# The first weight unit behind each norm of the second block works on inputs without the root

## The reference

```python
def rmsnorm(x, g):
    y = x * lax.rsqrt(jnp.mean(x * x, axis=-1, keepdims=True) + NORM_EPS)
    return y * g
def modulate(x, g, shift, scale):
    return rmsnorm(x, g) * (1 + scale) + shift
# layer 0
x = x + 0.5*gt1 * swiglu(modulate(x, g1, sh1, sc1), ffn1_wi, ffn1_wo)   # and ctx alike
x = x + gt2 * conformer_conv(modulate(x, g2, sh2, sc2), ...)            # 31 taps, LayerNorm, swish
x = x + 0.5*gt3 * swiglu(modulate(x, g3, sh3, sc3), ffn2_wi, ffn2_wo)
# layer 1: the same, with windowed attention in place of the convolution;
# its last two sublayers update x alone
return rmsnorm(x, final_g)
```

## Time and profile before

| | us |
|---|---|
| median of three runs | 3041.43 (3038.14 to 3042.28) |
| the profiled execution | 3040.12 |
| its span | 3038.3 |
| TensorE busy | 2990.5 (98%) |
| VectorE busy | 2131.6 (70%) |
| ScalarE busy | 1310.9 (43%) |
| DMA, mean over the span | 165 GB/s |

### The profile page before, as it was taken

One profiled execution on the slowest core, in us unless ns is written; L12 is line 12 of the kernel. 1 busy time (PEld: TensorE's weight loads), 2 busy tenths in 40 slices (PEclk: granted clock), 3 DMA queues, 4 the chain that ended last, 5 costly groups with the idle time before them and its releaser, 6 DMA issues.

```text
span 3038.3 us, 48548 instructions
## 1 busy us (share of the span) xinstructions
PE 2990.5 (98%) x20524; PEld 2699.5 (89%) x20524; DVE 2131.6 (70%) x3314; ACT 1310.9 (43%) x1972; POOL 2.0 (0%) x5
## 2 busy tenths in 40 slices
PE   9999999999999999999999999999999999998999
PEld 9999999999999999998888865788888888886999
DVE  6668767767878766666678788666765678567655
ACT  5455555455454555454222332432224222246544
POOL 0000000000000000000000000000000000000000
PEclk9999999999999999999999999999999999999999
DMA  6554554645654555543445445134442344420453
GB/s 233 191 172 170 172 181 176 225 164 202 220 199 170 172 195 182 185 148 130 167 178 194 171 146 179 70 139 167 190 162 101 146 168 189 152 98 29 167 181 112
DMA packets 87736, 500.71 MB, mean 165 GB/s; under 512 B 15200, under 2 KB 20192, under 8 KB 33120
## 3 DMA queue, kind: packets, MB, share of 16 engines
q1 hardware_dynamic: 84928, 492.73, 45.0%
q10 hardware_dynamic: 2592, 4.88, 0.5%
HBM read 493.92 MB, written 3.65 MB: 164 GB/s over the span
## 4 chain that ended last, share of the span: by engine, by line
PE 87%; DVE 7%; ACT 2%; DVEq 2%; issue 1%; DMA 1%; SPq 0%; ACTq 0%
PE ps L699 27%; PE ps L700 27%; PE ps L701 27%; DVE wl L1829 2%; DVE Pp L1821 1%; ACT wh L1324 1%; DVEq L2477 1%; DVE Hl L1821 1%; DVE XX L1821 1%; PE ps L983 0%; ACT Hh L1431 0%; PE ps L854 0%; PE ps L801 0%; DMA shifted<-u_rows 0%; PE ps L690 0%
## 5 line engine op out<-in xcount | busy, mean ns | idle before, releaser
L1829 DVE TENSOR_TENSOR wl<-raw,wh 128x1024 fp32r<-128x1024 f32 (+2 forms) x779 | 919.4, 1184 | 621.1 <-ACT wh L1324 619.6
L1324 ACT ACTIVATE wh<-raw 128x1024 fp32r<-128x1024 f32 (+2 forms) x779 | 794.1, 1026 | 1256.1 <-PE ps L701 1221.3
L699 PE MATMUL ps<-Fh,wh 128*128 128x256 f32 (+1 forms) x3280 | 994.0, 303 | 7.5 <-DVE wl L1829 3.0
L700 PE MATMUL ps<-Fl,wh 128*128 128x256 f32 (+1 forms) x3280 | 989.0, 302 | 0.0
L701 PE MATMUL ps<-Fh,wl 128*128 128x256 f32 (+1 forms) x3280 | 989.0, 302 | 0.0
L699 PE MATMUL ps<-Hh,wh 128*128 128x256 f32 (+1 forms) x2576 | 866.9, 337 | 12.2 <-DVE Hl L1821 7.8
L700 PE MATMUL ps<-Hl,wh 128*128 128x256 f32 (+1 forms) x2576 | 856.4, 332 | 0.0
L701 PE MATMUL ps<-Hh,wl 128*128 128x256 f32 (+1 forms) x2576 | 856.1, 332 | 0.0
L699 PEld LDWEIGHTS ps<-Fh,wh 128*128 128x128 f32 x3280 | 626.7, 191 | 33.9 <-issue 5.7
L701 PEld LDWEIGHTS ps<-Fh,wl 128*128 128x128 f32 x3280 | 626.8, 191 | 22.6
L700 PEld LDWEIGHTS ps<-Fl,wh 128*128 128x128 f32 x3280 | 626.9, 191 | 22.3
(11 more groups left out here) (300 smaller groups left out, 1846.1 us busy)
## 6 DMA issues: line engine op xcount, KB each, us to landing
raw<-in_units SPq DMA_DIRECT2D x349, 1024.0 KB, 4.8
raw<-in_ada SPq DMA_DIRECT2D x72, 1024.0 KB, 6.8
raw<-in_units SPq DMA_DIRECT2D x32, 768.0 KB, 4.2
shifted<-u_rows SPq DMA_DIRECT2D x16, 284.5 KB, 4.4
shifted<-u_rows ACTq DMA_DIRECT2D x16, 284.5 KB, 4.8
QK<-in_conds SPq DMA_DIRECT2D x3, 1024.0 KB, 7.5
raw<-in_units SPq DMA_DIRECT2D x10, 256.0 KB, 3.1
blocks<-in_taps SPq DMA_DIRECT2D x8, 320.0 KB, 7.9
```

Of the source, the lines that this page charges most:

```text
L699: nc.tensor.matmul(o, wh[:, u.par, kc, w], xh(kc), start=(kc == 0), stop=False)
L700: nc.tensor.matmul(o, wh[:, u.par, kc, w], xl(kc), start=False, stop=False)
L1324: nc.scalar.activation(tile_of(wh[:, u.par], t, n), raw_tile(u, t), ACT.Copy) \
L1829: V.tensor_tensor(tile_of(wl[:, u.par], t, n), raw_tile(u, t), tile_of(wh[:, u.par], t, n).bitcast(F32), ALU.subtract).then_inc(lo_done, 1)
```

## The change

At norms 10 to 14 the first unit runs on x * gain without the root and without the shift. The root depends on the token alone, that is on the column, and the shift on the feature alone, so W(x gain root + shift) = root * W(x gain) + W shift. `Hh` and `Hl` get 16 more columns per chunk (chunks 272 columns apart), of which two hold the shift, and `plain_unit` multiplies 258 columns of one stream at a time: 96 matmuls where both streams count. The product of the second stream goes to banks 5 and 6. The sums and the spread of the root stand between its chunks, and the fillers are gone. Afterwards `Hh` and `Hl` are rewritten with the full norm for the second unit, which runs by itself.

ScalarE forms the plain high parts (`plain_highs`) behind the squares of each output unit, VectorE the low parts (`plain_lows`) in the next output unit; chunks 4 to 6 stand behind the last update, where also the `lo` of `add_last` went, and chunk 7 behind the reciprocal. ScalarE copies the root from PSUM to `root_copy`, from which VectorE takes it. VectorE then reads the shift's product from column 256 (`read_shifts`) and multiplies the unit's result by the root (`times_root`, four pieces); ScalarE's `Silu`, or identity and `Tanh`, run with W shift as a bias per stream; for keys VectorE adds it. In the convolution TensorE does the taps of chunks 0 and 1 behind unit 2, and `first_mean` behind unit 3.

```diff
-        Hh = sb("Hh", [P, 2, C, T], F32R)
+        Hh_wide = sb("Hh_wide", [P, 2, C, T + 16], F32R)
...
+            def plain_unit(u, norm, n):
+                between = {(0, 0): lambda: sums(norm, False, n), (1, 0): lambda: sums(norm, True, n),
+                           (2, 1): lambda: spread_roots(4, number(norm), n)}
+                pe.wait_ge(lo_done, u.lo_done(1))
+                pe.wait_ge(banks_free[u.par], u.banks_free())
+                for kc in range(C):
+                    for t in range(2):
+                        if (kc, t) in between:
+                            between[kc, t]()
+                        if t == 0:
+                            pe.wait_ge(plain_there, plain_chunk(norm, kc))
+                        w = slice(P * t, P * t + P)
+                        for s in range(n // T):
+                            o = ps[:, plain_bank(u, t, s), 0:T + 2]
+                            nc.tensor.matmul(o, wh[:, u.par, kc, w], Hh_wide[:, s, kc, 0:T + 2], start=(kc == 0), stop=False)
+                            nc.tensor.matmul(o, wh[:, u.par, kc, w], Hl_wide[:, s, kc, 0:T + 2], start=False, stop=False)
+                            mm = nc.tensor.matmul(o, wl[:, u.par, kc, w], Hh_wide[:, s, kc, 0:T + 2], start=False, stop=(kc == C - 1))
...
             for j in range(C):
-                linear(Unit(K2_CONV + j), part(Hh, 512), part(Hl, 512), 512, ready=h_ready(3) if j == 0 else None)
+                if j == 0:
+                    plain_unit(Unit(K2_CONV), 10, 512)
+                else:
+                    linear(Unit(K2_CONV + j), part(Hh, 512), part(Hl, 512), 512, ready=h_ready(3) if j == 1 else None)
                 if j == 2:
+                    depthwise(0)
+                    depthwise(1)
+                if j == 3:
                     first_mean()
-                if j >= 1:
+                if j >= 3:
                     depthwise(j - 1)
...
-            two_units(Unit(K2_KV), part(Hh, 512), part(Hl, 512), 512, h_ready(6), 2, second=value_products)
+            plain_unit(Unit(K2_KV), 13, 512)
...
+            def plain_highs(norm_i, n, kcs):
+                for kc in kcs:
+                    for s in range(n // T):
+                        ins = nc.scalar.activation(Hh[:, s, kc, :], (Xx, Xc)[s][:, kc, :], ACT.Copy, scale=scale_of(norm_i, kc, s))
+                    ins.then_inc(plain_high, 1)
...
+                if norm_i is not None:
+                    act.wait_ge(rb_done, number(norm_i))
+                    nc.scalar.activation(root_copy[:, 0:n], ps[:, 4, 0:n], ACT.Copy).then_inc(root_copied, 1)
                 for kc in range(C):
+                    if norm_i is not None and kc < C - 1:
+                        act.wait_ge(plain_read, (norm_i - 10) * (C - 1) + kc + 1)
...
+                        if kind == "G" and fi > 4 and g == 0 and i == 0:
+                            dve.wait_ge(mm_done, u.mm_done(1))
+                            read_shifts(u, n)
+                            times_root(Ss, u, 0, n).then_inc(rooted, 1)
+                            times_root(Pp[:, u.par], u, 1, n).then_inc(banks_free[u.par], 1)
+                            lo(u.later(2), 0)
...
+                if j == 0:
+                    dve.wait_ge(mm_done, u.mm_done(1))
+                    read_shifts(u, 512)
+                    dve.drain()
+                    for t in range(2):
+                        stt(shifted_by[:, :, t], shifted_by[:, :, t], 0.5, tiny[:, 32 + C * t:33 + C * t].to_broadcast([P, 2]), ALU.mult, ALU.add)
+                    times_root(Ss, u, 0, 512)
+                    times_root(Tt[:, u.par], u, 1, 512).then_inc(banks_free[u.par], 1)
+                    dve.drain().then_inc(rooted, 1)
                 lo(u.later(2), 0)
-                dve.wait_ge(banks_free[u.par], u.read_out())
+                if j == 0:
+                    dve.wait_ge(turned, 1)
```

More of the change, by code:

```diff
@@ L410, in build @@
                              "oh2_done", "o2_done"))
+        plain_high, plain_there, plain_cols, plain_read = (sem(n) for n in ("plain_high", "plain_there", "plain_cols", "plain_read"))
+        rooted, turned, root_copied, gated = sem("rooted"), sem("turned"), sem("root_copied"), sem("gated")
         stored = sem("stored")
@@ L893, in ffn @@
                     for j, (kind, i, u) in enumerate(units):
-                        if kind == "G" and norm is None and g == 0 and i < 2:
+                        if kind == "G" and fi > 4 and g == 0 and i == 0:
+                            plain_unit(u, norm_of(fi), n)
+                        elif kind == "G" and fi > 4 and g == 0 and i == 1:
+                            linear(u, part(Hh, n), part(Hl, n), n, ready=h_ready(hn))
+                        elif kind == "G" and norm is None and g == 0 and i < 2:
                             if i == 0:
@@ L1880, in norm, with norm_parts @@
             def norm(norm_i, n, hn, gain, shift, next_unit=None):
-                rms(norm_i, n, next_unit)
-                norm_parts(n, hn, gain, shift)
-            def norm_parts(n, hn, gain, shift, next_unit=None):
+                dve.wait_ge(std_done, norm_i + 1)
+                V.reciprocal(Rr[:, 0:n // 4], Rr[:, 0:n // 4]).then_inc(rs_done, 1)
+                plain_lows(norm_i, n, (C - 1,))
+                lo(next_unit, 1)
+                dve.wait_ge(root_copied, norm_i - 9)
+                norm_parts(n, hn, gain, shift, root=root_copy)
+            def norm_parts(n, hn, gain, shift, next_unit=None, root=ps[:, 4, :]):
                 def product(kc):
@@ L1989, in ffn @@
                             continue
+                        if kind == "G" and fi > 4 and g == 0 and i == 0:
+                            done = fi * FC
+                            dve.wait_ge(mm_done, u.mm_done(1))
[4 more added lines that the diff above has]
+                            dve.drain()
+                            dve.wait_ge(tanh_done, done + 1)
+                            for s in range(n // T):
+                                p = Pp[:, u.par, s * T:(s + 1) * T]
+                                ins = stt(p, p, shifted_by[:, s, 1:2], Tt[:, u.par, s * T:(s + 1) * T], ALU.add, ALU.mult)
+                            ins.then_inc(gated, 1)
+                            lo(u.later(2), 1)
+                            dve.wait_ge(fh_done, done + 1)
+                            if n == T:
+                                o, p, h = Fl[:, 0, i, :], Pp[:, u.par, 0:n], Fh[:, 0, i, :]
+                            else:
+                                o, p, h = Fl[:, 0:2, i, :], two(Pp[:, u.par, :]), Fh[:, 0:2, i, :]
+                            V.tensor_tensor(o, p, h.bitcast(F32), ALU.subtract).then_inc(f_done, 1)
+                            continue
                         lo(u.later(2), 0)
@@ L1992, in ffn @@
                             vector_step(o)
+                        if last and i >= 1 and 10 <= after < 15:
+                            plain_pair(after, n, i - 1)
                         if last and i >= 2 and not summed_on_pe(after):
```

156 lines of the change are left out of this document (122 added, 34 removed).

## The result

| | before | changed |
|---|---|---|
| median of 12 runs, us | 3041.37 (3038.14 to 3042.78) | 3046.93 (3044.73 to 3048.84) |
| ratio | | 1.0019 (95%: 1.0010 to 1.0028) |
| profiled execution, us | 3040.12 | 3047.57 |
| its span | 3038.3 | 3045.8 |

The prediction was 3034.1, in a range of 3027 to 3043. The kernel became 5.6 us slower, 12.8 us above the forecast. In the changed file the three products of `linear` are L726 to L728 (L699 to L701 before), those of the plain unit L831 to L833, `lo` is L1926, `hi` L1375, the high part of the full norm L1504, the root products of the first unit L1958.

A forecast was written before the change was run, and what follows sets the result against it. It took TensorE's time lost around norms and VectorE in the convolution as bounds. Terms 4.3 + 4.3 + 1.9 + 0 - 3.2 = 7.3 us, taken from the median 3041.43, gave 3034.1, range 3027 to 3043.

The forecast's parts named there:

- the accounting of the units: Around norms 11 and 12: two units' products need 21.8 of 31 us, 8.4 lost; the split costs 0.7 a unit.
- likeliest case: Whole kernel: the forecast's own outcome, 3029.5 to 3037 us, chance 0.52.
- Norms 11 and 12: Third unit starts about 26 us behind the last product instead of 30.2; gain 4.3 at each norm.
- Norm 13: Rotation waits 3 us on VectorE but starts at 2713.9 against 2715.83; gain 1.9 (1.4 to 2.5).
- Norm 14: One stream: third unit starts at 2849.8 against 2849.61; gain 0 (-1 to +1).
- Norm 10: Norm and convolution: new work in VectorE's queue delays the second weight pass by 3.3; loss 3.2 (1.5 to 6).
- A: Rival: VectorE's and ScalarE's chain from last update to third unit's weights is longer at all five norms; 3048.6; chance 0.13.
- B: Rival, no change: smaller gains (3039) or a lower clock after TensorE's convolution idle (3044); 3037 to 3045; chance 0.25.
- its mild case: Convolution: the clock falls only briefly after TensorE's idle; some 3 us of slower work fits in 4 us of slack.
- C: Rival, better: the convolution loses nothing and the chain is 0.3 shorter; 3029.4; chance 0.10.
- The forecast's own sum: Norms 10 to 14 and the convolution: 4.3 + 4.3 + 1.9 + 0 - 3.2 = 7.3 us gained.
- the mark of being wrong: Third unit waiting for weights much beyond 26 us, or VectorE idle within the convolution, would show the forecast wrong.

## Why the prediction was wrong

**The failed step** is in the accounting of the units: "a unit is 48 products 0.227 apart (10.9)", and the only price of the wider chunks is "+0.7 a unit, paid at norms 10 to 13". The change was priced at the five norms; the 66 units between them that read `Hh` and `Hl` stayed at the old pace without a sentence on it, although its own description has `Hh` and `Hl` with 16 more columns a chunk. That is a cost of zero that was never argued. Measured: 389 to 393 and 395 ns a product, +10.0 alone in the kernel before, 8.6 inside the changed one. With it taken out, the changed kernel stands at 3038.3, inside the range of the prediction, but 4.2 above its 3034.1 and outside its likeliest case (3029.5 to 3037). What is left of the error is in norms 13 and 14 and in the granted clock, below.

**Norms 11 and 12** (predicted 4.3 each): right. The third unit starts 26.1 behind the last product, as said (26). By the passes norm 11 gained 4.2 and norm 12 3.7 in the kernel with norms 11 to 13. Its steps, counted from the end of the last product's slot (1955.67; the prediction's 1950.0): spread 5.65 (5.66), first root product 7.4 (7.6), end of the first unit 14.5 (14.7), of the second 25.6 (25.6), last low part's end 22.8 (22.45), weight pass 24.8 (24.6), third unit 26.1 (25.9). Chunks come every 1.92, not 1.855. A first root product 0.2 earlier, and ScalarE's table and weight copy in 2.46 instead of 2.56, make up for most of it. ScalarE's copy is what ends last, as said: VectorE's root products took 1.4 instead of 1.65, and it then waited 0.52 for that copy.

**Norm 13** (predicted 1.9): the mechanism was as said, the size not settled. Rotation, then VectorE:

```profile
2721.19 2.08 PE L1249 MATMUL ps<-Gb,ro 128*128 128x512 f32 x2 [2.71 <-DVE Gb L2741]
2722.27 1.20 PE L726 MATMUL ps<-Hh_wide,wh 128*128 128x256 f32 x1
```

```profile
2718.51 1.41 DVE L1958 TENSOR_TENSOR Gb<-ps,Gb 128x256 f32<-128x256 f32 x4
2719.99 1.14 DVE L2741 TENSOR_SCALAR Gb<-Gb,shifted_by 128x256 f32<-128x256 f32 x4
```

A wait of 2.71 (predicted 3). Rotation starts 28.8 behind the last product, against 30.9, a gain of 2.1. But the wait is followed by a low granted clock (the first product behind it takes 1.20), and again later in the attention. What is left by the passes runs from 0.8 gained (norms 11 to 13 against 11 and 12) to 0.7 lost; the losses are in the kernels whose clock stayed low for 6.8 us at once. The prediction left the clock out at this wait.

**Norm 14** (predicted 0, -1 to +1): a loss of 2.0. Chunks come 1.52 apart, not 1.455, which is most of the 0.7 by which the last low part is later than predicted:

```profile
2853.38 0.48 DVE L1918 SCALAR_TENSOR_TENSOR Hl_wide<-Pp,MOD,Hh_wide 128x256 fp32r<-128x256 f32 x1 [0.64 <-ACT Hh_wide L1504]
...
2855.84 1.22 DVE L1926 TENSOR_TENSOR wl<-raw,wh 128x1024 fp32r<-128x1024 f32 x1 [1.24 <-ACT wh L1375]
```

```profile
2857.12 0.39 PE L726 MATMUL ps<-Hh_wide,wh 128*128 128x256 f32 x1 [2.24 <-DVE wl L1926]
```

The third unit starts 20.8 behind the last product (20.1 before), and the idle time of 2.24, where 0.49 had stood, is followed by a granted clock of 0.5 from 2857.65 on, for 3.4 us. The later third unit is 0.7 of the 2.0, the rest is what the passes lose behind it; the kernel whose clock didn't fall here lost the 0.7 alone.

**Norm 10** (predicted -3.2): 2.5 to 2.7, by two errors that cancel. The second weight pass starts at 1780.41, 3.0 later relative to the norm (predicted 3.3), and TensorE waits for chunk 1's rows, and the clock falls to 0.51 as it had at the stage's end:

```profile
1800.85 6.34 PE L1183 MATMUL ps<-shifted,blocks 128*32 128x512 f32 x32 [5.97 <-DMA shifted<-u_rows]
...
1819.75 1.13 PE L1191 MATMUL ps<-QK,ones 128*128 128x512 f32 x2 [1.24 <-DVE QK L2599]
```

It idles 5.97 (predicted 7), then finishes before VectorE needs it, as said. The tap order is worth 1.6 to 2.7, not 0.1, and the new work in VectorE's queue costs about 5, not 3.3. That the term came out is luck.

**The rivals.** A (a longer VectorE and ScalarE chain, 3048.6) is close in its number and wrong in its cause: the third units and the rotation came within 0.5 us of the forecast at every norm. B had the clock, and behind TensorE's hole in the convolution it fell for 6.8 us without reaching VectorE, as in its mild case; what the clock cost was at norms 13 and 14, which B didn't name. C fails: the convolution did lose. The forecast's own sum, with what was measured: 4.2 + 3.7 + 0.7 - 2.0 - 2.6 = 4.0 gained, 1.5 lost at the end of the first block and 8.6 lost to the pitch: 3047.5 against 3046.9. The 8.6 is itself a difference from the changed kernel's median, so what the sum tests is 3038.9 against the 3038.3 without the pitch, and its terms come from several kernels' single profiles. What was given as the mark of being wrong, a third unit well beyond 26 us or idle time on VectorE in the convolution (none over 0.46), wasn't there; the sum failed in a place that had no mark.

## What to carry to other kernels

When a buffer's shape changes, even by padding that nothing reads, count every instruction that reads it and price it anew: 3168 products by 5 ns, some 16 us, outweighed what five norms gained, even with 5 us given back by the products of 256 columns. Such a cost is in no wait; compare the mean duration of one form of instruction before and after (389 to 395 ns) before any chain of waits. And when buffers are moved, look at where every other operand lands, since what counts here is the distance between two of them.
